# The opening of a hybrid decoder layer: the first modulation in quarters, token scales from one product

## The reference

```python
cond = jax.nn.silu(c)
mod = cond @ w_ada[layer] + b_ada[layer]             # (1024) @ (1024 x 6144)
shift1, scale1, gate1, shift2, scale2, gate2 = jnp.split(mod, N_MOD, axis=-1)
h = modulate(rms_norm(x), shift1, scale1)            # h * (1 + scale) + shift
y = hybrid_mixer(h, ...)                             # h @ w_in, two linear-attention groups, @ w_out
x = x + gate1 * y
h = modulate(rms_norm(x), shift2, scale2)
y = jnp.square(jax.nn.relu(h @ w_mlp1)) @ w_mlp2
x = x + gate2 * y
return rms_norm(x, final_norm_g)
```

## Time and profile before

| | us |
|---|---|
| median of 3 runs | 1147.47 (1147.12 to 1149.27) |
| the profiled execution | 1147.12 |
| its span | 1145.4 |
| TensorE busy | 1127.8 (98%) |
| VectorE busy | 873.8 (76%) |
| ScalarE busy | 612.9 (54%) |
| GpSimd busy | 495.2 (43%) |

### The profile page before, as it was taken

How to read it: one execution, slowest core, us unless ns; L and a number is a source line. 1 busy time by engine, 2 the same in 40 slices (tenths; PEclk the granted TensorE clock), 3 DMA queues, 4 the chain that set the end, 5 groups by cost and what they waited for, 6 DMA issues and landing times.

```text
span 1145.4 us, 15528 instructions
## 1 busy us (share of the span) xinstructions
PE 1127.8 (98%) x5483; PEld 935.0 (82%) x5483; DVE 873.8 (76%) x1035; ACT 612.9 (54%) x933; POOL 495.2 (43%) x318
## 2 busy tenths in 40 slices
PE   7999999999999999999999999999999999999997
PEld 6888787888888888888888888888888888888886
DVE  6898987779788776379975675567796875966776
ACT  7763554766656675356555455545664433524425
POOL 1021023235353345347542434243576665765750
PEclk9899999999999999999999999999999999999999
DMA  9767477445363457513255533554425537437203
GB/s 355 273 223 259 161 176 220 101 129 157 101 185 95 144 184 232 191 56 127 100 169 175 184 130 121 173 184 161 152 74 189 193 96 268 154 129 283 66 1 147
DMA packets 162949, 186.71 MB, mean 163 GB/s; under 512 B 7605, under 2 KB 119353, under 8 KB 159929
## 3 DMA queue, kind: packets, MB, share of 16 engines
q1 hardware_dynamic: 160472, 179.44, 47.0%
q0 software_dynamic: 2400, 6.29, 2.8%
HBM read 138.51 MB, written 40.89 MB: 157 GB/s over the span
## 4 chain that ended last, share of the span: by engine, by line
PE 93%; DMA 2%; DVE 2%; issue 1%; SPq 1%; ACT 1%; POOL 0%; DVEq 0%; ACTq 0%
PE unit_bank L1807 19%; PE unit_bank L2262 9%; PE unit_bank L2263 9%; PE unit_bank L2264 9%; PE small_bank L2263 9%; PE small_bank L2264 9%; PE small_bank L2262 9%; PE small_bank L1807 4%; PE unit_bank L2095 4%; PE unit_bank L2097 3%; PE unit_bank L2096 3%; DMA ada_slot<-in_w_ada_dram 2%; PE small_bank L1846 1%; PE small_bank L1949 1%; DVE ada_acc L2363 1%
## 5 line engine op out<-in xcount | busy, mean ns | idle before, releaser
L1039 POOL TENSOR_TENSOR wr_lo<-quarter,wr_hi 128x512 fp32r<-128x512 f32 x122 | 196.7, 1625 | 174.3 <-ACT wr_hi L1596 174.1
L2262 PE MATMUL unit_bank<-op_hi,wr_hi 128*128 128x512 f32 x452 | 176.6, 391 | 0.5 <-issue 0.5
L2264 PE MATMUL unit_bank<-op_hi,wr_lo 128*128 128x512 f32 x452 | 175.9, 389 | 0.0
L2263 PE MATMUL unit_bank<-op_lo,wr_hi 128*128 128x512 f32 x452 | 175.8, 389 | 0.0
L2262 PE MATMUL small_bank<-op_hi,wr_hi 128*128 128x512 f32 x448 | 174.5, 389 | 0.0
L2264 PE MATMUL small_bank<-op_hi,wr_lo 128*128 128x512 f32 x448 | 174.3, 389 | 0.0
L2263 PE MATMUL small_bank<-op_lo,wr_hi 128*128 128x512 f32 x448 | 174.3, 389 | 0.0
L1596 ACT ACTIVATE wr_hi<-wr_full 128x512 fp32r<-128x512 f32 x90 | 56.8, 631 | 174.2 <-DVE wr_full L3046 169.3
L3046 DVE TENSOR_TENSOR wr_full<-quarter,quarter 128x512 f32<-128x512 f32 x90 | 89.3, 993 | 55.5 <-PE small_bank L2264 23.0
L1596 ACT ACTIVATE wr_hi<-quarter 128x512 fp32r<-128x512 f32 x136 | 82.9, 626 | 88.9 <-PE unit_bank L2264 50.1
L1807 PE MATMUL unit_bank<-a_hi,w_hi 128*128 128x512 f32 x304 | 121.0, 398 | 0.0
(11 more groups left out here) (387 smaller groups left out, 2374.4 us busy)
## 6 DMA issues: line engine op xcount, KB each, us to landing
quarter<-in_w_mlp_dram SPq DMA_DIRECT2D x128, 256.0 KB, 4.0
hidden_scratch<-hid SPq DMA_DIRECT2D x98, 256.0 KB, 2.4
ada_slot<-in_w_ada_dram SPq DMA_DIRECT2D x48, 512.0 KB, 6.4
op_full<-hidden_scratch SPq DMA_DIRECT2D x21, 1024.0 KB, 4.8
pair_quarter<-in_w_in_dram SPq DMA_DIRECT2D x32, 256.0 KB, 3.3
piece_x<-t_scratch SPq DMA_DIRECT2D x16, 512.0 KB, 4.9
piece_y<-t_scratch SPq DMA_DIRECT2D x32, 256.0 KB, 3.4
raw<-in_w_out_dram SPq DMA_DIRECT2D x16, 512.0 KB, 4.6
```

The source lines that it names most:

```text
L1039: pool.tensor_tensor(wr_lo[slot][:, :, :], split_source(n), wr_hi[slot][:, :, :].bitcast(F32), ALU.subtract).then_inc(wr_lo_pool, 1)
L2262: pe.matmul(dst, wh, ah, start=opens, stop=False, skip_group_check=True)
L2263: pe.matmul(dst, wh, al, start=False, stop=False, skip_group_check=True)
L2264: mm = pe.matmul(dst, wl, ah, start=False, stop=k == KH - 1, skip_group_check=True)
```

## The change

It rebuilds the opening up to units 0 and 1. The first modulation comes in four quarters: quarter `q` holds depth tiles 2q and 2q+1, that is 256 columns of the shift and 256 of the scale, in four pieces of 256 depth rows. Two DMAs load a piece. The sum over depth becomes a row of 512 in partition 0 of a PSUM bank: for quarter 0 by TensorE alone (eight products with `cond` as a one-column stationary operand), for the others VectorE sums three pieces (six passes of 512 columns) and TensorE adds the fourth piece and VectorE's sum. ScalarE copies the row, four small products turn it into four columns, and VectorE adds the bias. The token scales of a half come from one product of ones with the diagonals, left in a PSUM bank, in place of the 64 products; VectorE multiplies `xT` by the scale column and these token scales in one pass (`scaled_input`). The shift is added in the rounding (`high_input`) and in the low half. SyncE waits before most loads of the opening until the one four places earlier has landed. ScalarE alone copies tiles 4 to 7 of `xT`. Each engine's order is rewritten to match; counters of later stages are adjusted.

```diff
+BY_VECTOR = (0, 3, 3, 3)
@@ SyncE
                 if last:
-                    sp.wait_ge(ada_added, last[0] + 1)
+                    sp.wait_ge(ada_added, 4 * (last[0] // 4) + 4 if last[0] < 16 else last[0] + 1)
...
+                    for kk in range(2):
+                        sp.dma_start(ada_slots[slot][:, kk * HALF:(kk + 1) * HALF].rearrange("p (a n) -> p a n", a=2),
+                                     src[:, kk, :, h * 2 * P:(h + 1) * 2 * P]).then_inc(ada_loaded[slot], 8 * 2)
...
-            for t in range(3, TT):
-                load_x(t)
+            load_x(3)
+            sp.wait_ge(x_loaded[0], 16)
+            load_unit(0, 0, w_in, 0, GLR)
+            sp.wait_ge(x_loaded[1], 16)
+            load_unit(1, 1, w_in, 0, GK)
+            sp.wait_ge(x_loaded[2], 16)
+            load_ada(0)
+            sp.wait_ge(x_loaded[3], 16)
+            load_ada(1)
+            sp.wait_ge(raw_loaded[0], 16)
+            load_ada(2)
+            sp.wait_ge(raw_loaded[1], 16)
+            load_ada(3)
...
-            for n in range(8):
+            for t in range(4, TT):
+                landed_ada(t - 4)
+                load_x(t)
+            for n in range(4, 16):
+                if n < 8:
+                    sp.wait_ge(x_loaded[n], 16)
+                else:
+                    landed_ada(n - 4)
                 load_ada(n)
-            load_unit(0, 0, w_in, 0, GLR)
-            load_unit(1, 1, w_in, 0, GK)
-            for n in range(8, 20):
+            load_unit(2, 0, w_in, 0, GQ)
+            for n in range(16, 20):
                 load_ada(n)
@@ ScalarE
+            roots(0)
+            for u in range(2):
+                high_of(u)
+            copy_row(0)
+            act.wait_ge(read["x"], 8)
+            for t in range(4, TT):
+                copy_x(t)
+                square_x(t)
+                if t == 5:
+                    for k, half in INPUTS[0:2]:
+                        high_input(k, half)
+            roots(1)
+            copy_row(1)
+            for k, half in INPUTS[2:6]:
+                high_input(k, half)
+            copy_row(2)
+            for k, half in INPUTS[6:10]:
+                high_input(k, half)
+            copy_row(3)
+            for k, half in INPUTS[10:]:
+                high_input(k, half)
+                if (k, half) == (5, 1):
+                    high_of(2)
@@ TensorE
+            def depth_sums(q, pieces, last=False):
+                dst = QUARTER_BANK[q][0:1, :]
...
+                for kp in pieces:
+                    wait_ada(pe, 4 * q + kp)
+                    for kk in range(2):
+                        k = 2 * kp + kk
+                        mm = pe.matmul(dst, cond[:, k:k + 1], ada_slots[ADA_SLOT[4 * q + kp]][:, kk * HALF:(kk + 1) * HALF],
+                                       start=k == 2 * BY_VECTOR[q], stop=last and k == KT - 1 and not BY_VECTOR[q],
+                                       skip_group_check=True)
+                if last and BY_VECTOR[q]:
+                    pe.wait_ge(modulated, sum(n > 0 for n in BY_VECTOR[:q + 1]))
+                    mm = pe.matmul(dst, ones[:, 0:1], ada_acc[:, 4 * q * P:4 * (q + 1) * P], start=False, stop=True,
+                                   skip_group_check=True)
...
+            def token_scales(half):
+                pe.wait_ge(diag_ready, half + 1)
...
+                product(SB[2 + half][:, :], ones[:, :], tok(t1, half)).then_inc(scaled_x, TT)
+            depth_sums(0, (0,))
+            token_scales(0)
+            depth_sums(0, (1, 2, 3), True)
+            turn_x(4)
+            depth_columns(0)
+            for t in range(5, TT):
+                turn_x(t)
+            first_units(0, 0)
+            token_scales(1)
+            depth_sums(1, (3,), True)
+            depth_columns(1)
+            first_units(0, 1)
+            first_units(1, 0)
+            depth_sums(2, (3,), True)
+            first_units(1, 1)
+            depth_columns(2)
+            first_units(2, 0)
+            depth_sums(3, (3,), True)
+            first_units(2, 1)
+            depth_columns(3)
+            first_units(3, 0)
+            first_units(3, 1)
@@ VectorE
+            def first_inputs(q, half, between=None):
+                for k in (2 * q, 2 * q + 1):
+                    scaled_input(k, half)
+                if between:
+                    sum_quarter(*between)
+                for k in (2 * q, 2 * q + 1):
+                    low_input(k, half)
+            pack_gate()
+            low_weights_first(1)
+            finish_first(0)
+            first_inputs(0, 0)
+            sum_quarter(1, (0,))
+            diagonals(1)
+            sum_quarter(1, (1,))
+            sum_quarter(1, (2,))
+            first_inputs(0, 1)
+            sum_quarter(2, (0,))
+            finish_first(1)
+            first_inputs(1, 0, (2, (1,)))
+            sum_quarter(2, (2,))
+            first_inputs(1, 1, (3, (0,)))
+            finish_first(2)
+            first_inputs(2, 0, (3, (1,)))
+            sum_quarter(3, (2,))
+            first_inputs(2, 1)
+            finish_first(3)
+            first_inputs(3, 0)
+            first_inputs(3, 1)
```

More of the change, by code:

```diff
@@ L638, in ada_piece, with input_number @@
             g, q = divmod(n, 16)
-            return (g, q % 8, q // 8) if g == 0 else (g, q // 2, q % 2)
+            return (g, q % 4, q // 4) if g == 0 else (g, q // 2, q % 2)
+        def input_number(k, half):
+            return 4 * (k // 2) + 2 * half + k % 2 + 1
+        INPUTS = [(k, half) for q in range(4) for half in range(2) for k in (2 * q, 2 * q + 1)]
+        QUARTER_BANK = (UB[3], SB[0], SB[1], SB[0])
         def split_source(n):
@@ L651, in wait_ada @@
             slot = ADA_SLOT[n]
-            e.wait_ge(ada_loaded[slot], 16 * ADA_SLOT[:n + 1].count(slot))
+            e.wait_ge(ada_loaded[slot], 16 * sum((2 if m < 16 else 1) for m in range(n + 1) if ADA_SLOT[m] == slot))
         block = ctx.enter_context(nc.Block())
@@ L1143, in _, with copy_row, roots @@
             act.wait_ge(consts, 11)
[L1144 to L1147, removed]
+            def copy_row(q):
+                act.wait_ge(modulated_late, q + 1)
+                act.activation(ada_acc[0:1, 4 * q * P:4 * (q + 1) * P], QUARTER_BANK[q][0:1, :], ACT.Copy).then_inc(small_ready, 1)
+            def roots(g):
                 act.wait_ge(squared, 4 * (g + 1))
@@ L1982, in turn_x @@
                          ).then_inc(filled["x"], 1)
-            for t in range(TT - 3):
+            for t in range(4):
                 if t == 2:
@@ L2011, in _ @@
[L2011 to L2021, removed]
+            def token_scales(half):
+                pe.wait_ge(diag_ready, half + 1)
+                if half == 0:
+                    pe.wait_ge(read["rows"], 1)
+                product(SB[2 + half][:, :], ones[:, :], tok(t1, half)).then_inc(scaled_x, TT)
@@ new lines, in first_units @@
+            def first_units(q, half):
+                for k in (2 * q, 2 * q + 1):
+                    for u in range(2):
+                        half_unit(u, u, half, a_hi, a_lo, split_ready(0), (k,))
+            depth_sums(0, (0,))
[8 more added lines that the diff above has]
+            depth_sums(1, (3,), True)
@@ L2047, in stage @@
                     elif name == "P0":
-                        kind, count = (("ada", 3), ("ada", 4), ("ada", 1), ("ada", 2))[b]
-                        pe.wait_ge(read[kind], count)
+                        if b < 2:
+                            pe.wait_ge(read["ada"], 4 - b)
+                        else:
+                            pe.wait_ge(normalised, input_number(KT - 1, b - 2))
                     else:
@@ new lines, in low_input, with sum_quarter @@
+            def low_input(k, half):
+                dve.wait_ge(split_hi, input_number(k, half))
+                dve.wait_ge(ada_added, 4 * (k // 2) + 4)
+                dve.scalar_tensor_tensor(tok(a_lo[:, k], half), tok(a_full[:, k], half), col(mod, k),
+                                         tok(a_hi[:, k], half).bitcast(F32), ALU.add, ALU.subtract).then_inc(lo_dve, 1)
+            def sum_quarter(q, pieces):
+                acc = ada_acc[:, 4 * q * P:4 * (q + 1) * P]
+                for kp in pieces:
+                    wait_ada(dve, 4 * q + kp)
+                    for kk in range(2):
+                        k = 2 * kp + kk
+                        src = ada_slots[ADA_SLOT[4 * q + kp]][:, kk * HALF:(kk + 1) * HALF]
+                        if k == 0:
+                            ins = dve.tensor_scalar(acc, src, col(cond, 0), None, ALU.mult)
+                        else:
+                            ins = dve.scalar_tensor_tensor(acc, src, col(cond, k), acc, ALU.mult, ALU.add)
+                        if k == 2 * BY_VECTOR[q] - 1:
+                            ins.then_inc(modulated, 1)
+                        else:
+                            then(ins)
```

155 lines of the change are left out of this document (46 added, 109 removed).

## The result

The changed kernel takes 1173.82 us (median of 4 runs, 1173.73 to 1174.36) against 1147.3 us for the kernel before beside it; the ratio is 1.023 with a 95% interval of 1.0218 to 1.0243, so it is slower by 26.5 us. The forecast was 1171.4. The profiled span is 1172.1 us, 26.7 more than before.

The account below looks back on a forecast made before the run. TensorE, busy 98% of the span, was taken as the bound, so only the end of its opening waits mattered: 1147.1 + 19.5 (later end) + 1.8 (next stage) + 3 (clock) = 1171.4 us, range 1156 to 1183.

Parts of the forecast that it names:

- The mark: End of units 0 and 1, where step "z" starts and TensorE hardly waits again: 58.8 us before, 78.3 forecast.
- parts 2 and 3: Opening: TensorE's added products give VectorE its first scale at 23.2 us; VectorE then needs 36 us of passes.
- part 4: Waits between engines in the opening: quarter columns at 41.3, 55.8 and 70.4 us, the mark 19.5 us later.
- A turn: One quarter's loop over VectorE, TensorE and ScalarE, from columns to the next columns: 14.6 us.
- part 3: VectorE's opening passes: 36 us from 23.2, so the mark would be at 60.4 us even without any wait.
- part 6: TensorE's clock in the opening: one fall behind a pause and part of a second, +3 us, bounds 0 and 14.6.
- half speed behind every long pause: Rival: opening matmuls and depth products behind three or four pauses double, 8 to 15 us, 1176 to 1184; chance 0.2.
- part 5: Next stage: VectorE starts 1.75 us before the mark instead of 3.6, and its delay reaches TensorE: +1.8 us.
- part 1: Opening loads: hidden up to piece 11; pieces 12 to 15 wait for quarter 1's columns, still landing in time; hold free.
- the looser loop: Rival: cheaper depth products (0.43 us) or engines getting ahead put the mark at 60.4 to 72.1; 1150 to 1165, chance 0.17.
- faster: Rival: units 0 and 1 run behind each quarter's loads, the mark 8.4 us earlier, 1139 to 1141; chance 0.04.
- unchanged: Rival: VectorE's passes packed and 2 us quicker than priced, the mark within 2.3 us of 58.8; chance 0.03.

Follow-up runs that it names:

- run 1: The changed kernel plus 12, 8, 16, 8 and 10 matmuls with unused results filling TensorE's five pauses ahead of matmul groups: 1170.45 us.
- run 3: The changed kernel with TensorE turning the next quarter's row into columns ahead of half 1's ten matmuls, for quarters 2 and 3: 1166.95 us.
- run 4: The changed kernel with both reorderings: ScalarE rounds half 1 before copying the next row, TensorE makes columns before half 1's matmuls: 1162.04 us.
- run 5: The changed kernel without SyncE's waits for the load four places earlier, load order and free-buffer waits kept: 1173.79 us.
- run 7: The changed kernel with VectorE summing two pieces instead of three in quarters 1 to 3, and TensorE taking two: 1179.05 us.
- run 2: The changed kernel with ScalarE rounding half 1 of quarters 1 and 2 ahead of copying the next quarter's row: 1168.1 us.
- run 10: The changed kernel with both ScalarE's and TensorE's reorderings, plus 8, 6 and 4 filler matmuls ahead of half 0 of quarters 1 to 3: 1162.76 us.
- run 6: The changed kernel with VectorE copying tiles 4 to 7 of xT and ScalarE only squaring them: 1176.41 us.

## Why the prediction was right, point by point
The time was inside the range and 2.4 us above the forecast; the mechanism was the forecast's likeliest. Its terms:

- **The mark and the loss behind VectorE's start** (parts 2 and 3) held. First columns: 23.2 forecast, 23.4 to 23.7 in runs 1, 3, 4, 5 and 7, whose depth products began at full clock, 25.21 in the changed kernel, where they began at half. The next columns came 17.4 us later, where 18.1 was forecast. A depth product costs what a product of 128 columns does, as run 7 and the rows show.
- **The waits between** (part 4) held in place and kind: roots 2.5 us as forecast, low halves waiting for ScalarE, columns waiting for TensorE (3.05). A turn was priced at 14.6; at full clock (run 1) it is 15.1, twice. Runs 2 to 4 and 10 shorten it by reordering alone. That VectorE's 36 us of passes are a bound by themselves (part 3, mark at 60.4) was never tested: with both orders and the clock full the loop still takes 11.1, more than the 9.8 of passes.
- **The clock** (part 6) was the term that was mis-sized: +3 us forecast, 7.0 measured. Against run 1 the turns lost 1.5 and 1.9 us and the last part 2.0; the first columns lost 1.5 against the five runs at full clock there. The five pauses themselves were forecast well (3.6, 2.5, 4.1, 2.5 and 3.0 us; measured 3.33, 2.13, 4.18, 2.08 and 2.83), but I had counted one fall behind them and part of a second. It fell behind three, and also at 14 us, where I expected none. *The Trainium skill's rule ("TensorE: Matmul & The Clock Gate", Part 1), that idleness halves the clock and only sustained work restores it, was given to a rival. The trace agrees with it in kind: half clock behind the pauses of 3.33, 4.18 and 2.83 us, full clock again before the end of each group.* That rival, with half speed behind every long pause for 8 to 15 us, was right for three of the five pauses and too high in price. The truth lies between it and the forecast.
- **Behind the mark** (part 5) failed for this kernel: +1.8 forecast, -0.7 measured. VectorE was to start its next stage 1.75 us before the mark. It started 3.3 before, nearly as in the kernel before (3.6), because TensorE's last 20 matmuls began at half clock and held the mark back, and TensorE was idle for 0.25 us in the 50 us behind the mark, as before. Where the lead was 1.8 us (runs 1, 3, 4 and 10), and in run 6, TensorE did lose time behind the mark, 0.4 to 1.7 us in two waits. The chain of waits leads from both not to a full VectorE but to a load that part 5 leaves out. The weights of unit 3 are queued on SyncE behind modulation pieces that wait for quarter 3's columns; ScalarE waits for them with all its later work, VectorE waits for ScalarE, and so does TensorE some 12 and 24 us behind "z". In run 10:
```profile
78.66 1.06 ACT L1125 ACTIVATE w_hi<-raw 128x1024 fp32r<-128x1024 f32 x1 [5.04 <-DMA raw<-in_w_in_dram]
...
85.74 1.23 DVE L2727 SCALAR_TENSOR_TENSOR t<-t,cum 128x1024 f32<-128x1024 f32 x1 [2.45 <-ACT t L1301]
...
86.25 0.50 PE L1823 MATMUL unit_bank<-a_hi,w_hi 128*128 128x512 f32 x1 [1.25 <-ACT t L1241]
```
  TensorE's first wait grows with the lateness of these weights: none in run 4 (3.9 us behind "z"), then 0.17 us in run 1 (4.1), 0.36 in run 6 (4.3), 0.96 in run 3 (4.9) and 1.25 in run 10 (5.2); the second is 0.43 to 0.46 us in all five. So no run shows the 1.8 us that VectorE's late start was to cost. The spans behind "z" differ by more than these waits, and the rest stays open: each is one execution, and executions of the kernel before alone differ by up to 3.3 us.
- The sum came out near because misses cancel: 4 us too little for the clock and 1 us too little for the turns stand against 2.5 too much behind the mark. The closeness of the total is in part luck.
- **The loads** (part 1) held up to the mark: hidden up to piece 11, idle from 34 to 42, nobody late for pieces 12 to 15 (run 10), the hold worth nothing (run 5). Behind it the weights of unit 3 were late, as said.

Of the rivals, the looser loop is excluded by the price of a depth product (0.86 us, run 7) and by VectorE's waits of 3.05 us for columns, faster and unchanged by the time.

No run beat the kernel before. The best form of the new opening, run 4, stays 1.3% above it (1.0129, interval 1.0112 to 1.0146).

## What to carry to other kernels
When work is cut into quarters so that it can follow its loads, write down one turn of the loop as a sum over all engines in their program order; what counts is that sum, not the busiest engine in it (9.8 us of passes became a turn of 16.8). Then look in each engine's list for an instruction that the next turn waits for and that stands behind one that only this turn needs: two such swaps gave back 11.8 us here. Pauses on TensorE can be paid twice, once as pauses and again at half clock in the work behind them: in the changed kernel those of 2.83 to 4.18 us were, and the two of 2.1 us were not. When two kernels are compared by their profiles, compare the stretch that the edit acts on; a start that the clock made 1.5 us earlier or later can pass for an effect of the edit.

## What the runs showed that I had not expected
- A pass of GpSimd and certain passes of VectorE get in each other's way: 2.85 us instead of 0.68 for a low half (two inputs), 2.77 instead of 0.75 for a sum's first pass (one tensor input), each ending 0.55 us behind GpSimd's; and the GpSimd pass that started during a VectorE sum (two tensors and a scalar) took 3.28 us instead of 2.36, while that sum kept its 1.28. The kernel before had it already: three sums from 60.45 us on took 5.67 us, where three take 3.8, beside a GpSimd pass that began at 60.25. The durations fit the reading that whichever pass starts first delays the other until it ends. *The Trainium skill, "GPSIMD Engine Reference", Specifications, names contention with VectorE instructions that have two inputs in SBUF or use both ports; the trace agrees for passes with two inputs. Whether the one-input pass uses both ports, no run here shows.*
- TensorE's clock was at half at 14 us in some profiles (the changed kernel, runs 2 and 10, first columns at 25.2, 26.3 and 25.7) and full in others (runs 1, 3, 4, 5 and 7, 23.4 to 23.7), with the same code up to there but for the hold in run 5. It is a difference of 1.5 to 3 us that no edit is known to have made.
